# Down projection of a SwiGLU block: four plain columns and two seven-product pairs instead of two and three, and the four token sums on GpSimd

## The reference

```python
D_MODEL, D_FF = 1024, 2816

def swiglu(x, w_gate, w_up, w_down):
    return (jax.nn.silu(x @ w_gate) * (x @ w_up)) @ w_down

def second_block(x, ...):
    h = jnp.concatenate([meta, x], axis=1)
    for l in range(DEPTH):
        h = h + 0.5 * swiglu(rmsnorm(h, norm_gains[l, 0]), ffn_w_gate[l, 0], ffn_w_up[l, 0], ffn_w_down[l, 0])
        h = h + mixer(...)
        h = h + 0.5 * swiglu(rmsnorm(h, norm_gains[l, 2]), ffn_w_gate[l, 1], ffn_w_up[l, 1], ffn_w_down[l, 1])
    return rmsnorm(h, final_norm)[:, N_META:]
```

## Time and profile before

| | before |
|---|---|
| median of 3 runs | 3677.41 us |
| lowest, highest | 3674.63, 3678.92 us |
| profiled execution, its own time | 3678.66 us |
| its span, first to last instruction | 3676.6 us |
| TensorE busy | 98% of the span |
| VectorE, ScalarE, GpSimd busy | 75%, 47%, 25% |

### The profile page before, as it was taken

One profiled execution on the slowest core, in us unless ns is written; L12 is line 12 of the kernel. 1 busy time (PEld: TensorE's weight loads), 2 busy tenths in 40 slices (PEclk: granted clock), 3 DMA queues, 4 the chain that ended last, 5 costly groups with the idle time before them and its releaser, 6 DMA issues.

```text
span 3676.6 us, 64756 instructions
## 1 busy us (share of the span) xinstructions
PE 3598.6 (98%) x24230; PEld 3270.6 (89%) x24230; DVE 2757.8 (75%) x3944; ACT 1722.6 (47%) x3001; POOL 934.1 (25%) x757
## 2 busy tenths in 40 slices
PE   8999999999999999999999999999999999999999
PEld 5778888677888889999998999999999999899998
DVE  4677763566777389995667699989998466769997
ACT  3544332345433255554235555555555423646554
POOL 1121110012111025540003035543553000304552
PEclk9999999999999999999999999999999999999999
DMA  3122233212222323332110233232323212032333
GB/s 118 47 75 69 97 97 102 84 47 75 70 97 95 105 86 98 104 99 89 64 64 30 69 103 98 98 110 92 103 93 104 84 58 70 18 104 87 98 98 109
DMA packets 107211, 313.35 MB, mean 85 GB/s; under 512 B 30048, under 2 KB 32224, under 8 KB 106688
## 3 DMA queue, kind: packets, MB, share of 16 engines
q1 hardware_dynamic: 106384, 304.60, 25.7%
q0 software_dynamic: 560, 5.09, 0.4%
HBM read 307.48 MB, written 2.10 MB: 84 GB/s over the span
## 4 chain that ended last, share of the span: by engine, by line
PE 87%; issue 6%; DVE 3%; POOL 2%; ACT 2%; DMA 1%; SPq 0%; POOLq 0%; DVEq 0%; ACTq 0%
PE acc L3155 34%; PE misc L3749 29%; PE acc L3770 5%; PE acc L3324 3%; PE misc L3155 2%; PE misc L4164 1%; PE acc L3666 1%; PE acc L3713 1%; PE acc L3234 1%; POOL probs_hi L2959 1%; PE acc L3864 1%; PE acc L3307 1%; PE acc L3786 1%; PE misc L3941 1%; PE misc L3365 1%
## 5 line engine op out<-in xcount | busy, mean ns | idle before, releaser
L795 ACT CAST w_hi<-stage 128x1024 fp32r<-128x1024 f32 x290 | 303.1, 1045 | 713.8 <-PE acc L3155 584.7
L1690 DVE TENSOR_TENSOR w_lo<-stage,w_hi 128x1024 fp32r<-128x1024 f32 x290 | 396.2, 1366 | 206.2 <-ACT w_hi L795 200.3
L3155 PE MATMUL acc<-x_hi,w_hi 128*128 128x264 f32 (+1 forms) x1984 | 544.3, 327 | 4.2 <-DVE w_lo L1690 3.5
L3155 PE MATMUL acc<-x_lo,w_hi 128*128 128x264 f32 (+1 forms) x1984 | 539.9, 325 | 0.0
L3155 PE MATMUL acc<-x_hi,w_lo 128*128 128x264 f32 (+1 forms) x1984 | 538.2, 324 | 0.0
L2288 DVE TENSOR_TENSOR w_lo<-s_blocks,w_hi 128x512 fp32r<-128x512 f32 x416 | 410.1, 987 | 13.4 <-ACT w_hi L1258 10.2
L2288 DVE TENSOR_TENSOR w_lo<-stage,w_hi 128x512 fp32r<-128x512 f32 (+1 forms) x392 | 352.6, 903 | 38.8 <-ACT w_hi L1258 37.9
L3155 PEld LDWEIGHTS acc<-x_hi,w_hi 128*128 128x128 f32 x1984 | 332.3, 189 | 45.5 <-issue 8.7
L3749 PE MATMUL misc<-t_hi,w_hi 128*128 128x264 f32 x1280 | 367.5, 287 | 1.5 <-ACT u_part L1285 1.5
L3749 PE MATMUL misc<-t_hi,w_lo 128*128 128x264 f32 x1280 | 363.3, 284 | 0.0
L3749 PE MATMUL misc<-t_lo,w_hi 128*128 128x264 f32 x1280 | 362.3, 283 | 0.0
(11 more groups left out here) (495 smaller groups left out, 9202.8 us busy)
## 6 DMA issues: line engine op xcount, KB each, us to landing
stage<-weights SPq DMA_DIRECT2D x568, 512.0 KB, 3.3
rotary_decay<-tables POOLq DMA_DIRECT2D x2, 2048.0 KB, 8.3
x<-x_in SPq DMA_DIRECT2D x4, 512.0 KB, 8.0
lse_rows<-lse_columns SPq DMA_DIRECT2D x128, 0.5 KB, 2.0
rotary_masks<-tables SPq DMA_DIRECT2D x2, 784.0 KB, 4.5
out<-x SPq DMA_DIRECT2D x8, 132.0 KB, 1.9
out<-x SPq DMA_DIRECT2D x8, 124.0 KB, 1.8
params<-params SPq DMA_DIRECT2D x2, 279.0 KB, 3.6
```

Of the source, the lines that this page charges most:

```text
L795: nc.scalar.copy(whi[(p + turn[0]) % 2][:, :], stage[p][:, :]).then_inc(hi_ready, 1)
L1690: nc.vector.tensor_tensor(wlo[w][:, :], stage[p][:, :], whi[w][:, :].bitcast(F32), ALU.subtract).then_inc(lo_ready, 1)
L3155: ins = mm(ps[:, b, 0:tn], ww, act_[:, kt, t0:t0 + tn], start=start and n == 0 and q == 0, stop=stop and n == last and q == 2)
```

## The change

The down columns 2 and 3 of the chunks 0 and 1 become plain columns, so that two pairs are left in each, columns 4 and 5 and columns 6 and 7. The plain columns `Da`, `Db` 2 and 3 stand ahead of the pairs on every engine. `f_sum` moves from VectorE's program to GpSimd's, where the four stand behind the `s_sums` of the chunk's last gate and up column and ahead of the `s_sums` of the first pair; the first of them waits for `gate_second` and `f_lo` of the column before (n = 7 or 15). On VectorE `gate_second(b)` and `f_lo(b)` stand ahead of the first `update`. In a pair, the sum of the first column's two token halves onto `x` becomes one instruction (`x1`, 528 elements) instead of two (`x11`, `x12`), and `c22` goes into `u3_part` instead of `gate`.

```diff
 def paired(j):
-    return [PAIRED + 3 * j + m for m in range(3)] if j < 2 else []
+    return [PAIRED + 2 * j + m for m in range(2)] if j < 2 else []
 def paired_column(n):
-    return KT * ((n - PAIRED) // 3) + 2 + 2 * ((n - PAIRED) % 3)
+    return KT * ((n - PAIRED) // 2) + 4 + 2 * ((n - PAIRED) % 2)
...
         names += [("Da", 8 * j + 1), ("Db", 8 * j), ("Db", 8 * j + 1)]
+        for c in (2, 3) if j < 2 else range(2, KT):
+            names += [("Da", 8 * j + c), ("Db", 8 * j + c)]
         for n in paired(j):
...
-                    for c in range(2) if j < 2 else ():
+                    for c in range(4) if j < 2 else ():
                         read("Db", KT * j + c)
                         ring(STRIP2["d", KT * j + c] + 4)
...
                     if j < 2:
-                        hi_block()
-                        hi_block()
                         f_hi_of_pair(b)
-                        hi_block()
-                        ev.up(2)
+                        for _ in range(7):
+                            hi_block()
+                        ev.up(4)
...
                     if j < 2:
                         xh0 = xhr.up(4) - 4
+                        gate_second(b)
+                        f_lo(b)
+                        lo_block()
+                        update(KT * j)
                         f_sum_lo(2, xh0)
                         lo_block()
-                        f_sum_lo(0, xh0)
-                        gate_second(b)
+                        update(KT * j + 1)
                         lo_block()
-                        f_sum_lo(1, xh0)
-                        update(KT * j)
+                        for c in (2, 3):
+                            lo_block()
+                            f_sum_lo(c - 2, xh0)
+                            update(KT * j + c)
+                            lo_block()
...
+                def f_sum(j, a):
+                    if a == 0:
+                        pool.wait_ge(pair_sum, sum_at(q, "ug2", KT * (j + 1) - 1))
+                    else:
+                        pool.wait_ge(xn_made, t_count(q, 4 + 4 * j + a))
+                    if a == 0:
+                        pool.wait_ge(ff_ready, FF2 + FT * q + KT * ((q + 1) // 2) + KT * (j + 1))
+                    left, right = ((1, 0), (2, 1), (2, 0), (3, 2))[a]
+                    nc.gpsimd.tensor_tensor(whole_part(a), whole_part(left), whole_part(right), ALU.subtract).then_inc(xn_made, 1)
...
                 for n in CHAIN2:
                     s_sums(n)
+                    for j in range(2):
+                        if n == CHUNKS2[j][1]:
+                            for a in range(4):
+                                f_sum(j, a)
...
                     down_half("Db", KT * j + 1, s1)
+                    for c in (2, 3) if j < 2 else ():
+                        s = next_slot()
+                        down_half("Da", KT * j + c, s)
+                        down_half("Db", KT * j + c, s)
```

More of the change, by code:

```diff
@@ L117 @@
 F_SUMS = ("S1", "S3", "S2", "A22")
+FF2 = LAYERS * FT
 F_RESTS = ("S2", "S1", "S3", "A22")
@@ L164, in pair_steps @@
             gates += [("u2", n), ("u3", n), ("p1", behind(n))]
-            sums += [("c11", n), ("x11", n), ("c22", n), ("ug1", n), ("x22", n), ("c12", n), ("x12", n)]
+            sums += [("c11", n), ("c22", n), ("ug1", n), ("x22", n), ("c12", n), ("x1", n)]
     return {k: i + 1 for i, k in enumerate(sums)}, {k: i + 1 for i, k in enumerate(gates)}
@@ L1289, in u3 @@
                     if RANK2[n]:
-                        act.wait_ge(pair_sum, sum_at(q, "c22", before(n)))
+                        act.wait_ge(pair_sum, sum_at(q, "x22" if before(n) >= PAIRED else "c22", before(n)))
                     nc.scalar.copy(U3B[:, :], banks2(n)[0]).then_inc(pair_gate, 1)
@@ L2322, in c11 @@
                     if RANK2[n]:
-                        dve.wait_ge(pair_sum, sum_at(q, "x22" if before(n) >= PAIRED else "ug1", before(n)))
+                        dve.wait_ge(pair_sum, sum_at(q, "x1" if before(n) >= PAIRED else "ug1", before(n)))
                     nc.vector.tensor_tensor(GS[:, 0:HALF], banks2(n)[2], P1B[:, RANK2[n] % 2, :], ALU.add).then_inc(pair_sum, 1)
@@ L2342, in c12 @@
                     if RANK2[n]:
-                        dve.wait_ge(pair_sum, sum_at(q, "x12" if before(n) >= PAIRED else "ug2", before(n)))
+                        dve.wait_ge(pair_sum, sum_at(q, "x1" if before(n) >= PAIRED else "ug2", before(n)))
                     dve.wait_ge(pair_gate, gate_at(q, "u2", n))
@@ L2352, in onto_x @@
                 def onto_x(name, n):
-                    c = paired_column(n) % KT + (name in ("ug1", "x22"))
-                    xm = x[:, c, 0:HALF] if name in ("x11", "ug1") else x[:, c, HALF:TALL]
+                    c = paired_column(n) % KT
                     if name == "ug1":
                         dve.wait_ge(blk_done, base + PLACE2["A22", n] + 1)
-                        part = banks2(n)[0]
-                    else:
-                        dve.wait_ge(pair_sum, sum_at(q, "c" + name[1:], n))
-                        part = GS[:, HALF:TALL] if name == "x12" else GS[:, 0:HALF]
+                        xm, part = x[:, c + 1, 0:HALF], banks2(n)[0]
+                    elif name == "x22":
+                        dve.wait_ge(pair_sum, sum_at(q, "c22", n))
+                        xm, part = x[:, c + 1, HALF:TALL], U3B[:, :]
+                    else:
+                        dve.wait_ge(pair_sum, sum_at(q, "c12", n))
+                        xm, part = x[:, c, :], GS[:, :]
                     nc.vector.scalar_tensor_tensor(xm, part, 0.5, xm, ALU.mult, ALU.add).then_inc(pair_sum, 1)
@@ L2422, in ffn2 @@
                     for n in range(a, b + 1):
-                        sums = j < 2 and n == b
                         c11(n)
@@ L3739, in product @@
                     pe.wait_ge(blk_lo, base + i + 1)
-                    if n >= PAIRED and (n - PAIRED) % 3 == 0 and name in F_SUMS:
-                        pe.wait_ge(xl_ready, xl0 + 2 * KT + 4 + 4 * ((n - PAIRED) // 3) + F_RESTS.index(name) + 1)
+                    if n >= PAIRED and (n - PAIRED) % 2 == 0 and name in F_SUMS:
+                        pe.wait_ge(xl_ready, xl0 + 2 * KT + 4 + 4 * ((n - PAIRED) // 2) + F_RESTS.index(name) + 1)
                     if n == PLAIN2 and name in ("S1", "S2", "S3", "A22"):
```

30 lines of the change are left out of this document (3 added, 27 removed).

## The result

The changed kernel takes **3716.55 us** (median of 4 runs, 3714.68 to 3720.35) against 3678.16 us before on the same chip: a ratio of 1.0102, 95% interval 1.0089 to 1.0114. It is 38 us slower, and 21 us slower than forecast. The profiled execution took 3716.89 us in all, its span is 3715.1 us, which is 38.5 more than before.

What follows compares the result with a forecast made beforehand. TensorE, busy 98% of the span, was taken as the bound. Per chunk end 1.46 - 2.65 + 3.5 = +2.3 us, eight +18.5, on 3678.66 gives 3697.2, less 1.25 for the median: 3696 us, range 3683 to 3714.

Steps and rivals of the forecast that it cites:

- The direction and the main mechanism: Slower: at each chunk end TensorE's Da 2 waits for update(0), held up by GpSimd's token sums and turns with VectorE.
- The matmuls: At each chunk end TensorE does 360 matmuls instead of 348, twelve more at 0.122 us: +1.46 us.
- The token sums: Each sum of 1056 elements on GpSimd was taken as 2.5 us, with 2.13 and 2.65 as ends.
- The stall: TensorE starts Da 2 at each chunk end at about 1439.15 instead of 1435.65: +3.5 us.
- The walk: Step-by-step times at one chunk end, from sum 0 at 1421.1 to update(0) ending at 1439.1.
- Nothing for the matmuls behind the stall: The sum for a chunk end had no term for slower TensorE matmuls after the wait at Da 2.
- rival 3: TensorE's matmuls run slower after every stall of 3.5 us: 15 us more, 3711 us; chance 0.15.
- The first pair's waits: TensorE's lost time in the first pair of each chunk end, counted as all given back: -2.65 us.
- I find no further wait in the pairs: Behind the stall everything gains the same time, so TensorE has no more waits in the pairs; no time added.

Runs made afterwards that it cites:

- e1: The changed kernel with update(0) moved on VectorE ahead of gate_second(b), f_lo(b) and the w_lo of Db 2; 3679.33 us, ratio 1.0004.
- e2: The changed kernel with the four token sums back on VectorE at their old places, new columns and pairs kept; 3675.2 us, ratio 0.9994.
- e4: The changed kernel with GpSimd's weight sums of each chunk's first pair waiting until f_lo(b) is done; 3685.79 us, ratio 1.0024.
- e8: The changed kernel with six extra matmuls on constants on TensorE ahead of the wait for update(0); 3701.58 us, ratio 1.0068.
- e9: The changed kernel with token sums on VectorE, update(0) ahead of gate_second(b), and f_sum_lo(3) moved right behind f_sum_lo(1); 3674.72 us, ratio 0.9991.
- e3: The kernel before with only the four token sums moved to GpSimd, f_sum_lo(2) also waiting for the last sum; 3709.61 us, ratio 1.0086.

## Why the prediction was wrong, step by step

- **The direction and the main mechanism** were right. TensorE's wait is before `Da` 2, for `update(0)`, behind `gate_second`, `f_lo` and a `w_lo` which take turns with the weight sums (e1, e2 and e4 show each part).
- **The matmuls:** 96 more, +1.46 us a chunk end, as said.
- **The token sums:** taken as 2.5 us. From the end of the `w_lo` ahead of it (1425.34) to its own end (1427.67) the second sum needs 2.33 us, and with the 0.1 us by which its turn starts before that end, 2.43. By the Trainium skill, "GPSIMD Engine Reference", section 3.1, the proportional estimate was 2.32; the trace agrees within 5%.
- **The stall:** forecast +3.5 us, measured 3.13 in the mean. The walk put `Da` 2 at 1439.15; with the 1.28 us by which this chunk end comes later (1436.93 against 1435.65 in the earlier trace rows) that is 1440.43, and it starts at 1440.14. This term was 0.37 us too large, 3.0 us in eight.
- **Nothing for the matmuls behind the stall:** this is the step that failed. The prediction left them out of the sum and gave rival 3 a chance of 0.15, because no row before had a wait of that length; but that was no evidence for the other side either. The slow matmuls came in seven of eight places; with the eighth, the loss is 1.54 us in the mean and 12.3 us in all, where rival 3 said 15. e8 shows the cause and e4 that a wait of 0.93 us brings none. The Trainium skill, "TensorE: Matmul & The Clock Gate", section "Why this matters for your kernels", warns of idle gaps between bursts; the trace agrees, at waits of 3 us.
- **The first pair's waits, -2.65 us counted as all given back:** this term was too large. All pairs of a chunk end lost 3.13 us before and lose 1.00 now, so 2.13 is given back, and 4.2 us of the sum are missing. "I find no further wait in the pairs" was wrong: a rest (2.35 us) and the blocks stand beside GpSimd's weight sums of the *second* pair, and the next matmuls wait 0.59 us for a `w_lo`; the last product waits another 0.3 for VectorE's `u_part`. The walk had stopped at the first pair. e9 shows that this wait can be moved but hardly removed.
- **Not in the sum at all:** the start of the next chunk waits for `u_part` of ScalarE, 0.68 us where 0.33 stood before in most places, 0.45 more in the mean, another 3.6 us. All kernels with two pairs have it (4.1 to 4.8 us in 8), so it comes with the pairs, not with GpSimd's sums. What exactly makes it longer was not tried and stays open.

With the measured terms a chunk end is 1.46 + 3.13 + 1.54 - 2.13 + 0.45 = 4.45 us, eight are 35.6, and the span grew by 38.5. Of the remaining 2.9 us, 1.1 were lost at 668 us, long before the first chunk end, where the granted clock from 668 to 672 us is 0.57 in the execution after and 1.00 in the one before; the rest is within what runs of one kernel differ by. The range ended at 3714: rival 3 in full would still have been inside, and so would the 7.8 us missing at the pairs and behind them. Both as measured, less the 3.0 us by which the stall was too large, come to 3713, and the 2.9 us outside the chunk ends carry it past.

## What to carry to other kernels

When a change makes a wait on the bounding engine, price what that engine does behind the wait too, above all when no row shows a wait of that length: here 3.13 us of wait brought 1.54 more, and a wait cut to a third brought nothing beyond itself. Walk the waits of a change through to the next piece of work that repeats, not only to the one removed. Work moved to GpSimd is not free for VectorE: what decides is which instructions of VectorE stand next to it and whether the bounding engine waits for one of them, and an instruction that reads PSUM and is due first belongs ahead of those that must take turns (e1: one line, 37 us).

## What the runs showed of the hardware beyond that

- The half pace behind an idle wait is not the same each time: waits of 2.96 to 3.26 us were followed by losses of 0.12 to 2.86 us, and the place with 0.12 had a wait of 3.12 us, longer than three of those with more than 1.3. The length of the wait doesn't tell which. In the place with 0.12 the granted clock stayed at 1.00 (2260 to 2264 us). In another the first matmuls still had it (1.00 from 2391.64 to 2392.03) and it fell only then (0.50 up to 2395). In e3 the clock fell at all eight waits (3.26 to 3.32 us). What decides was not found.
- A queue of GpSimd sums, each read from SBUF, and VectorE blocks take strict turns for as long as both have work: sums 2.88 us apart with a `w_lo` of 1.77 us (0.69 alone) in each, of which 0.55 us is work behind the sum's end.
- Plain fp32 matmuls of 256 columns on constants appear as two instructions each and take 0.42 us the pair, where a real one of 264 columns takes 0.122 us here.
